# Two token tiles routed ahead in a one-core layer of attention, retention and experts

## The chip, the cores and the metric

The kernel is one program on one core of a Trainium2 chip. Its time is what the device needs for one execution, in microseconds, and the figure given for a kernel is the median of several runs. The engines are TensorE (PE, with its weight loads PEld), VectorE (DVE), ScalarE (ACT), GpSimd (POOL) and SyncE (SP), which here only issues transfers. All synchronisation is by semaphores written out by hand.

## What is computed

One layer over 512 tokens of width 1024, in float32: a norm, one input projection, windowed attention with sinks (8 heads) beside chunkwise retention (4 heads), an output projection added to the input, a second norm, and a mixture of 16 gated experts. Each token picks one group of four experts and then two experts in that group:

```python
p_group = jax.nn.softmax(hf @ rg_w + rg_b, axis=-1)
g_prob, g_idx = lax.top_k(p_group, 1)
e_logits = (hf @ re_w + re_b).reshape(-1, N_GROUPS, EXPERTS_PER_GROUP)
sel = jnp.take_along_axis(e_logits, g_idx[:, :, None], axis=1)[:, 0]
top_p, top_i = lax.top_k(jax.nn.softmax(sel, axis=-1), TOP_K_IN_GROUP)
w = g_prob * top_p / jnp.sum(top_p, axis=-1, keepdims=True)
for e in range(N_EXPERTS):          # w becomes combine[:, e]
    y = (jax.nn.silu(h @ w_gate[e]) * (h @ w_up[e])) @ w_down[e]
    out = out + combine[:, e:e + 1] * y
```

A final norm follows. Ties go to the lower index.

## The kernel before

The 512 tokens are four tiles of 128 (T = 4). Every large product is done in three passes for float32 accuracy: each weight piece is split into a high part (ACT, `hi_ring`) and a low part (DVE, `lo_ring`), and `triple` (lines 1436 to 1438) multiplies high by high, high by low and low by high. Two rings of three slots hold the split weights; the raw weights arrive through SP in twelve slots of 1 MB.

The work up to the experts follows one list, `STEPS`: pairs (weight block g, token tile t). Each engine walks the same list and puts its own side work at the steps named by tables. The last eight steps alternate the two blocks of the second half of the output projection, tile by tile: (13,0), (14,0), (13,1), (14,1), ... (14,3). After block 14 of a tile, DVE adds the product to the residual (line 1190, `x2_ready`), ACT squares it and takes a root (lines 778 to 786), PE turns the four 128x128 pieces (`turn_x2`, line 1443), ACT copies them out of PSUM (line 769), and PE multiplies them by the router's weights (`logits`, line 1611, 20 columns: 4 groups and 16 experts). DVE scales the residual into the rows of the second norm (`norm2`, line 1138), and POOL writes them to DRAM (line 543), from where the experts' rows are gathered.

The routing itself starts when the logits of all four tiles stand. It is one chain over DVE, PE and POOL: DVE finds the best group and expert, takes it out, finds the second (`first_max`, lines 1232 to 1236, twice), forms the two one-hot tables (line 1249) and their sum `pair_any` (line 1253). PE multiplies that by a triangle of ones and by ones (lines 1694, 1696): the rank of each token in its expert's list. DVE reads the rank of each choice (lines 1259, 1261) and marks it in a row of 128 (`at_rank`, line 1263, four times). PE multiplies the marks by `records`, which hold the row numbers (line 1255), and so makes the lists of each expert (`list_fields`, line 1706). DVE moves them to `meta` (line 1267, `lists_ready`), and POOL gathers the rows of experts 0 and 1 from DRAM (line 550) once the lists and all four writes of rows are there (`h2_out`). PE turns the gathered rows, lists the weights of the choices the same way, and begins the first product of expert 0. Between these steps PE runs products that nobody reads, `keep_clock` (line 1451, 128x512), so that it stays busy.

The order is fixed by hand: each engine runs its instructions as the code writes them, and waits only on semaphores. The expert stage then repeats one step of six weight blocks for each expert.

## Time and profile before

| | us |
| --- | --- |
| median of 3 runs | 565.18 |
| lowest, highest | 564.01, 565.33 |
| the profiled execution, its own time | 563.17 |
| span of its instructions | 561.1 |
| routing, from the last logits to the first product of expert 0 | 240.92 to 258.42 |

| engine | busy us | share of the span |
| --- | --- | --- |
| PE | 541.8 | 97% |
| DVE | 422.4 | 75% |
| ACT | 354.9 | 63% |
| POOL | 121.9 | 22% |

The span runs from the first to the last instruction; 2.07 us of the profiled execution lie outside it. The share of PE counts the products that nobody reads, so that a busy PE in the routing is no sign of useful work. In the chain of waits each row is the time until the next step of the chain starts.

### The profile page before, as it was taken

To read this page: it belongs to the slowest core of one execution; us is meant where nothing else is said; L and a number is where in the kernel's file an instruction comes from. 1 tells how busy PE (TensorE), PEld (TensorE's weight loads), DVE (VectorE), ACT (ScalarE), POOL (GpSimd) and SP (SyncE) were. 2 spreads that over 40 slices of the span, in tenths; PEclk is the share of its full clock that TensorE was granted. 3 is DMA by queue.
4 is the path that set the end of the run, shared out by engine and by line. 5 is a ranking of instruction groups with operands and counts; after the bars stand their busy time and mean duration, and the time that the engine had idled before them with its cause. 6 is when DMAs were issued, how large, how long until landed. Compare 5 with 4: busy or idle time off the path is not lost.

```text
span 561.1 us, 7892 instructions
## 1 busy us (share of the span) xinstructions
PE 541.8 (97%) x2679; PEld 439.7 (78%) x2680; DVE 422.4 (75%) x574; ACT 354.9 (63%) x472; POOL 121.9 (22%) x109
## 2 busy tenths in 40 slices
PE   4999999999999999988999999999999999999995
PEld 3988777777877888867888888888888888888883
DVE  3563599555856742486888898888988898888986
ACT  5563554780335352443788787788778788787854
POOL 2360000000000000020441334323442334420420
PEclk9999999999999999997999999999999999999998
DMA  8999122323020237859999999999999999999595
GB/s 291 375 304 387 33 73 76 75 77 76 0 76 0 77 113 265 292 202 323 347 387 372 370 369 373 374 346 364 356 390 373 357 365 376 381 364 373 124 210 182
DMA packets 71963, 144.02 MB, mean 257 GB/s; under 512 B 3784, under 2 KB 13312, under 8 KB 71808
## 3 DMA queue, kind: packets, MB, share of 16 engines
q1 hardware_dynamic: 64816, 120.77, 61.9%
q0 software_dynamic: 7120, 22.90, 13.4%
q8 instruction: 15, 0.25, 0.2%
q14 instruction: 12, 0.10, 0.1%
HBM read 132.77 MB, written 14.30 MB: 262 GB/s over the span
## 4 chain that ended last, share of the span: by engine, by line
PE 91%; DVE 3%; DMA 2%; ACT 2%; issue 1%; POOL 0%; DVEq 0%; POOLq 0%
PE ps L1436 25%; PE ps L1438 25%; PE ps L1437 25%; PE ps L1443 7%; PE ps L1586 2%; PE ps L1572 2%; PE ps L1548 1%; PE ps L1611 1%; PE ps L1518 1%; DMA arena<-norm_g 1%; DMA arena<-h_dram,meta 1%; PE ps L1451 1%; PE ps L1456 1%; PE ps L1808 1%; PE ps L1706 0%
## 5 line engine op out<-in xcount | busy, mean ns | idle before, releaser
L1202 DVE TENSOR_TENSOR lo_ring<-arena,hi_ring 128x2048 fp32r<-128x2048 f32 x94 | 215.3, 2291 | 29.9 <-ACT hi_ring L859 28.7
L1436 PE MATMUL ps<-hi_ring,act_hi 128*128 128x512 f32 x576 | 232.7, 404 | 0.2 <-DVE act_lo L1127 0.2
L1438 PE MATMUL ps<-hi_ring,act_lo 128*128 128x512 f32 x576 | 225.6, 392 | 0.0
L1437 PE MATMUL ps<-lo_ring,act_hi 128*128 128x512 f32 x576 | 225.0, 391 | 0.0
L859 ACT ACTIVATE hi_ring<-arena 128x2048 fp32r<-128x2048 f32 x94 | 180.1, 1916 | 21.5 <-PE ps L1438 21.5
L1436 PEld LDWEIGHTS ps<-hi_ring,act_hi 128*128 128x128 f32 x576 | 108.7, 189 | 25.7 <-issue 5.0
L1438 PEld LDWEIGHTS ps<-hi_ring,act_lo 128*128 128x128 f32 x576 | 108.4, 188 | 23.7
L1437 PEld LDWEIGHTS ps<-lo_ring,act_hi 128*128 128x128 f32 x576 | 108.7, 189 | 20.3
L969 DVE SCALAR_TENSOR_TENSOR lo_ring<-arena,over,hi_ring 128x512 fp32r<-128x512 f32 x40 | 29.3, 748 | 30.4 <-ACT hi_ring L678 30.2
L581 POOL DMA_INDIRECT y_dram<-y,row_info x14 | 15.2, 1088 | 134.3 <-issue 134.3
L979 DVE TENSOR_TENSOR act_lo<-ps,act_hi 128x512 fp32r<-128x512 f32 x56 | 36.9, 683 | 8.2 <-ACT act_hi L708 5.1
L1443 PE MATMUL ps<-keep,arena 128*128 128x128 f32 x268 | 37.5, 281 | 3.0 <-DMA arena<-h_dram,meta 2.5
L1443 PEld LDWEIGHTS ps<-keep,arena 128*128 128x128 f32 x268 | 31.8, 144 | 8.9 <-DMA arena<-h_dram,meta 2.9
L575 POOL DMA_INDIRECT arena<-h_dram,gather_idx x14 | 33.2, 2375 | 25.4 <-issue 25.4
L540 POOL DMA_DIRECT2D arena<-norm_g x1 | 0.6, 558 | 155.9 <-PE ps L1443 155.9
L598 POOL COPY row_info<-meta 128x3 int32 (+1 forms) x16 | 29.3, 1833 | 4.0 <-DMA y_dram<-y,row_info 4.0
L678 ACT ACTIVATE hi_ring<-arena,over 128x512 fp32r<-128x512 f32 x40 | 27.6, 718 | 0.5 <-DMA arena<-w_in 0.5
L881 ACT ACTIVATE act_hi<-ps 128x512 fp32r<-128x512 f32 x15 | 9.0, 599 | 21.7 <-PE ps L1443 21.7
L876 ACT ACTIVATE act_hi<-ps 128x512 fp32r<-128x512 f32 x30 | 16.3, 597 | 10.0 <-PE ps L1443 10.0
L1436 PE MATMUL ps<-act_hi,hi_ring 128*128 128x256 f32 (+1 forms) x64 | 21.9, 343 | 0.2 <-DVE lo_ring L969 0.2
L1438 PE MATMUL ps<-act_hi,lo_ring 128*128 128x256 f32 (+1 forms) x64 | 21.5, 336 | 0.0
L1437 PE MATMUL ps<-act_lo,hi_ring 128*128 128x256 f32 (+1 forms) x64 | 21.5, 336 | 0.0
(229 smaller groups left out, 533.6 us busy)
## 6 DMA issues: line engine op xcount, KB each, us to landing
arena<-w_gate SPq DMA_DIRECT2D x32, 1024.0 KB, 14.9
arena<-w_up SPq DMA_DIRECT2D x32, 1024.0 KB, 15.4
arena<-w_down SPq DMA_DIRECT2D x32, 1024.0 KB, 14.7
arena<-w_in SPq DMA_DIRECT2D x16, 512.0 KB, 10.4
y_dram<-arena POOLq DMA_DIRECT2D x8, 512.0 KB, 11.5
res<-y_dram POOLq DMA_DIRECT2D x8, 512.0 KB, 9.7
arena<-w_in SPq DMA_DIRECT2D x3, 1024.0 KB, 12.7
res<-x SPq DMA_DIRECT2D x4, 512.0 KB, 8.0
```

Of the source, the lines that this page charges most:

```text
L575: by_length(e, lambda n: pool.indirect_dma_start(x_rows[b][0:n, :], None, h2_dram, bass.IndirectOffsetOnAxis(ap=gather_idx[0:n, b:b + 1], ...
L598: nc.gpsimd.tensor_copy(row_info[:, 4 * b:4 * b + 3], meta[:, bass.ds(e * 4, 3)]).then_inc(info_ready, 1)
L678: ins = nc.scalar.activation(dst, src, ACT.Copy, scale=gain)
L859: nc.scalar.activation(hi(N1 + n12), raw(n12), ACT.Copy).then_inc(hi_done, 1)
L876: nc.scalar.activation(xt[1 - b][0][:, 4 * a:4 * a + 4, :], ps[:, 4 + a, :].rearrange("p (k s) -> p k s", k=4), ACT.Copy).then_inc(x_hi, 1)
L969: ins = nc.vector.scalar_tensor_tensor(dst, src, gain, src_hi.bitcast(F32), ALU.mult, ALU.subtract)
L979: nc.vector.tensor_tensor(dst, ps[:, bank, :].rearrange("p (k s) -> p k s", k=4), src_hi.bitcast(F32), ALU.subtract).then_inc(done, 1)
L1202: nc.vector.tensor_tensor(lo(N1 + n12), raw(n12), hi(N1 + n12).bitcast(F32), ALU.subtract).then_inc(lo_done, 1)
L1436: nc.tensor.matmul(dst, a_hi, b_hi, start=start, stop=False)
L1437: nc.tensor.matmul(dst, a_hi, b_lo, start=False, stop=False)
L1438: return nc.tensor.matmul(dst, a_lo, b_hi, start=False, stop=stop)
L1443: ins = nc.tensor.transpose(ps[:, bank, i * P:(i + 1) * P], blk, ident)
```

## The change

Four things change, all in the stretch between the last projection and the first expert.

First, the routing is split in two. `gate(0, 2)` works on tiles 0 and 1 and stands on DVE in the step (13,3), before the last tile's products are done; `find_ranks(0, 2)` and the first marks follow before the last `norm2`. `gate(2, 4)`, `find_ranks(2, 4)` and the other marks follow for tiles 2 and 3. On PE the ranks go into two banks, 1 for the early tiles and 2 for the late ones, and the lists are added up tile by tile.

Second, the experts are chosen by one table: for each five fours of logits (the groups, and four experts in each group) all 4 by 4 differences are taken, compared with a table `later` that settles ties, and summed. A logit that none beats has count 0, the second has 1. Four times the group's count plus the expert's is below 2 for the two chosen.

Third, the products of one-hot tables and row numbers go from DVE to POOL (`index_records`), in four instructions instead of two. The first two stand ahead of the last write of rows on POOL's queue, the other two behind it.

Fourth, PE's fillers are 3, 2, 1 and 21 where they were 4, 4, 15, 6 and 14, and the last two before the first product are gone. The four splits of block 16's weights all stand behind the lists now; two of them stood before.

```diff
-            for t in range(T):
+            def index_records(i, t0, t1):
+                pool.wait_ge(hot_ready, i)
+                for f in range(2):
+                    nc.gpsimd.tensor_tensor(records[:, :, t0:t1, :, f], pair_tiles[:, :, t0:t1, :],
+                                            index_tiles[:, :, t0:t1, f:f + 1].to_broadcast([P, 2, t1 - t0, E]),
+                                            ALU.mult).then_inc(index_ready, 1)
+
+            for t in range(T - 1):
                 pool.wait_ge(h2_ready, t + 1)
                 pool.dma_start(h2_dram[t * P:(t + 1) * P, :], h2_buf[t % 2]).then_inc(h2_out[t % 2], 16)
+            index_records(1, 0, EARLY)
+            pool.wait_ge(h2_ready, T)
+            pool.dma_start(h2_dram[(T - 1) * P:, :], h2_buf[(T - 1) % 2]).then_inc(h2_out[(T - 1) % 2], 16)
+            index_records(2, EARLY, T)
...
+            def gate(t0, t1):
+                n = (t1 - t0) * GROUPS
+                shape = [P, n, PER_GROUP, PER_GROUP]
+                dve.wait_ge(lg_ready, T + t1)
+                for t in range(t0, t1):
+                    ins = nc.vector.scalar_tensor_tensor(lg[:, t, :, :].rearrange("p g j -> p (g j)"),
+                                                         ps[:, 6, t * N_LOGITS:(t + 1) * N_LOGITS], rms[:, T + t:T + t + 1],
+                                                         rbias[:, :], ALU.mult, ALU.add)
+                step_done(ins)
+                v = lg[:, t0:t1, :, :].rearrange("p t g j -> p (t g) j")
+                over_v = route[:, 0:n * 16].rearrange("p (g j i) -> p g j i", j=PER_GROUP, i=PER_GROUP)
+                step_done(nc.vector.tensor_tensor(over_v, v.unsqueeze(2).to_broadcast(shape),
+                                                  v.unsqueeze(3).to_broadcast(shape), ALU.subtract))
+                step_done(nc.vector.tensor_tensor(over_v, over_v, later_v.unsqueeze(1).to_broadcast(shape), ALU.is_gt))
+                step_done(nc.vector.tensor_reduce(beaten[:, t0:t1, :, :].rearrange("p t g j -> p (t g) j"), over_v,
+                                                  AX_X, ALU.add))
+                for t in range(t0, t1):
+                    ins = nc.vector.scalar_tensor_tensor(
+                        standing[:, t, :, :], beaten[:, t, 0, :].unsqueeze(2).to_broadcast([P, N_GROUPS, PER_GROUP]), 4.0,
+                        beaten[:, t, 1:, :], ALU.mult, ALU.add)
+                step_done(ins)
+                if t0 == 0:
+                    nc.vector.memset(pair_any[:, T * E:], 0.0)
+                flat = route[:, 320 + t0 * E:320 + t1 * E]
+                nc.vector.tensor_scalar(pair_any[:, t0 * E:t1 * E], flat, 2.0, None, ALU.is_lt).then_inc(pair_ready, 1)
+                pairs = [P, 2, (t1 - t0) * E]
+                nc.vector.tensor_tensor(pair_hot[:, :, t0 * E:t1 * E], flat.unsqueeze(1).to_broadcast(pairs),
+                                        order[:, 0:2].unsqueeze(2).to_broadcast(pairs), ALU.is_equal
+                                        ).then_inc(hot_ready, 1)
...
                 if (g, t) == (N1 - 2, T - 1):
-                    for piece in range(2):
-                        split_piece(N1 + 1, piece)
+                    gate(0, EARLY)
...
+            find_ranks(0, EARLY, ps[:, 1, 0:EARLY * E])
+            mark(0)
             norm2(T - 1)
-            dve.wait_ge(lg_ready, 2 * T)
...
+            gate(EARLY, T)
+            mark(1)
+            find_ranks(EARLY, T, ps[:, 2, 0:(T - EARLY) * E])
+            for t in range(EARLY, T):
+                mark(t)
             dve.wait_ge(lists_made, 1)
...
-            for piece in range(2, 4):
+            for piece in range(4):
                 split_piece(N1 + 1, piece)
...
+                if n == T + EARLY:
+                    pe.wait_ge(pair_ready, 1)
...
             turn_x2(2 * T - 1)
-            keep_clock(4, 0)
+            for t in range(EARLY):
+                nc.tensor.matmul(late, ones_b, pair_v[:, t:t + 1, :].to_broadcast([P, T - EARLY + 1, E]), start=(t == 0),
+                                 stop=False)
+            keep_clock(3, 0)
             logits(2 * T - 1)
-            keep_clock(15, 0)
...
+            pe.wait_ge(index_ready, 2)
+            pe.wait_ge(onehot_ready, 1)
+            list_fields(7, 0, 0, True, False)
+            pe.wait_ge(pair_ready, 2)
...
+            pe.wait_ge(index_ready, 4)
+            for t in range(EARLY, T):
+                pe.wait_ge(onehot_ready, t + 1)
+                ins = list_fields(7, 0, t, False, t == T - 1)
+            ins.then_inc(lists_made, 1)
+            keep_clock(21, 0)
...
             pe.wait_ge(weights_set, 2)
-            list_fields(3, 2).then_inc(weights_made, 1)
-            keep_clock(2, 0)
+            for t in range(T):
+                ins = list_fields(3, 2, t, t == 0, t == T - 1)
+            ins.then_inc(weights_made, 1)
```

The first place is DVE from the last tile's add to the last mark. `y_68` is the scratch of the routing (`route`), `over` holds the logits, `res` the residual, `arena` the rows of the second norm, `act_lo` the marks and records. Before:

```order
L1190 TENSOR_TENSOR res<-res,ps 128x512 [waits mm_done]
L975 RECIPROCAL stat<-stat 128x1 [waits root_done]
L1138 SCALAR_TENSOR_TENSOR arena<-res,stat,arena 128x1024 [waits h2_out1,dve_step]
L1241 SCALAR_TENSOR_TENSOR over<-ps,stat,rbias 128x20 [waits lg_ready]
L1241 SCALAR_TENSOR_TENSOR over<-ps,stat,rbias 128x20 x3
L1232 TENSOR_REDUCE y_68<-over 128x20 [waits dve_step]
...
L1259 TENSOR_TENSOR y_68<-y_68,ps 128x128 [waits rank_ready]
L1261 TENSOR_REDUCE y_68<-y_68 128x8 [waits dve_step]
L1263 TENSOR_TENSOR act_lo<-keep,y_68 128x256 [waits dve_step]
L1263 TENSOR_TENSOR act_lo<-keep,y_68 128x256 x3
```

And now, from the same add:

```order
L1270 TENSOR_TENSOR res<-res,ps 128x512 [waits mm_done]
L1209 TENSOR_TENSOR y_68<-y_68,ps 128x2x32 [waits hot_ready,rank_ready]
L1211 TENSOR_REDUCE y_68<-y_68 128x2x2 [waits dve_step]
L1214 TENSOR_TENSOR act_lo<-keep,y_68 128x2x128 [waits dve_step]
L992 RECIPROCAL stat<-stat 128x1 [waits root_done]
L1155 SCALAR_TENSOR_TENSOR arena<-res,stat,arena 128x1024 [waits h2_out1,dve_step]
L1179 SCALAR_TENSOR_TENSOR over<-ps,stat,rbias 128x20 [waits lg_ready]
L1179 SCALAR_TENSOR_TENSOR over<-ps,stat,rbias 128x20
L1185 TENSOR_TENSOR y_68<-over 128x160 [waits dve_step]
L1187 TENSOR_TENSOR y_68<-y_68,keep 128x160 [waits dve_step]
L1188 TENSOR_REDUCE y_68<-y_68 128x40 [waits dve_step]
...
```

The ranks and the mark of the early tiles now stand between the add and the last norm, and the gate of the late tiles is nine instructions where the gate of all four was nineteen.

The second place is PE from the last but one set of logits. `keep,res` is a turn of the residual, `rw,arena` the logits, `hi_ring` alone a filler, `y_68,count_w` the ranks, `act_lo` alone the lists. Before:

```order
L1451 MATMUL ps<-hi_ring 128x512 x4
L1611 MATMUL ps<-rw,arena 128x20 [waits x2_copied]
L1611 MATMUL ps<-rw,arena 128x20 x3
L1451 MATMUL ps<-hi_ring 128x512 x15
L1694 MATMUL ps<-y_68,count_w 128x80 [waits counts_set,pair_ready]
...
L1451 MATMUL ps<-hi_ring 128x512 x6
L1706 MATMUL ps<-act_lo 128x32 [waits onehot_ready] x8
L1451 MATMUL ps<-hi_ring 128x512 x14
```

And now:

```order
L1485 MATMUL ps<-hi_ring 128x512 x2
L1734 MATMUL ps<-act_lo 128x32 [waits onehot_ready,index_ready]
L1734 MATMUL ps<-act_lo 128x32
L1743 MATMUL ps<-y_68,count_w 128x48 [waits pair_ready]
...
L1734 MATMUL ps<-act_lo 128x32 [waits onehot_ready]
L1734 MATMUL ps<-act_lo 128x32
L1485 MATMUL ps<-hi_ring 128x512
L1734 MATMUL ps<-act_lo 128x32 [waits onehot_ready,index_ready]
...
L1485 MATMUL ps<-hi_ring 128x512 x21
```

Three fillers stand between the last logits and the lists where 21 stood, and seven more stand behind the lists. The lists wait for POOL (`index_ready`) as well.

The third place is POOL around the last write of rows. Now:

```order
L556 DMA h_dram<-arena 128x1024 [waits h2_ready] x3
L550 TENSOR_TENSOR act_lo<-y_68,norm_tmp 128x2x2x16 [waits hot_ready]
L550 TENSOR_TENSOR act_lo<-y_68,norm_tmp 128x2x2x16
L559 DMA h_dram<-arena 128x1024 [waits h2_ready]
L550 TENSOR_TENSOR act_lo<-y_68,norm_tmp 128x2x2x16 [waits hot_ready]
L550 TENSOR_TENSOR act_lo<-y_68,norm_tmp 128x2x2x16
L567 DMA arena<-h_dram,meta 128x1024 [waits lists_ready,h2_out1,h2_out0]
```

Before, the four writes followed each other with nothing between them and the gather.

## Rows read from the trace of the kernel before

**Rows 1.** The page's chain that ended last: shares of the span by engine.

```profile
PE 91%; DVE 3%; DMA 2%; ACT 2%; issue 1%; POOL 0%; DVEq 0%; POOLq 0%
```

**Rows 2.** The chain of waits through the routing: start us, us, what.

```profile
240.92 0.69 DVE over L1241 x4
...
245.22 0.21 PE ps L1694
...
247.01 1.08 PE ps L1706 x8
248.12 0.20 DVE meta L1267
...
249.19 4.65 DMA arena<-h_dram,meta
253.89 1.97 PE ps L1443 x8
255.86 1.52 PE ps L1706 x8
257.38 1.04 PE ps L1451 x2
258.42 0.43 PE ps L1436
```

**Rows 3.** Timeline of DVE: start us, us, line, operation, tiles, shapes, idle before.

```profile
233.24 0.68 DVE L964 TENSOR_TENSOR lo_ring<-arena,hi_ring 128x512 fp32r<-128x512 f32 x1
...
236.91 0.69 DVE L1190 TENSOR_TENSOR res<-res,ps 128x512 f32<-128x512 f32 x1 [0.33 <-PE ps L1438]
...
245.56 0.29 DVE L1259 TENSOR_TENSOR y<-y,ps 128x128 f32<-128x128 f32 x1
...
246.20 1.43 DVE L1263 TENSOR_TENSOR act_lo<-keep,y 128x256 fp32r<-128x256 f32 x4
```

**Rows 4.** Timeline of ACT at the last tile, and its first SiLU later.

```profile
238.39 0.30 ACT L786 ACTIVATE stat<-stat 128x1 f32<-128x1 f32 x1
239.17 0.59 ACT L769 COPY arena<-ps 128x512 f32<-128x512 f32 x1 [0.49 <-PE ps L1443]
...
265.04 0.60 ACT L904 ACTIVATE silu_g<-ps 128x512 f32<-128x512 f32 x1 [0.80 <-PE ps L1438]
```

**Rows 5.** Line 543 in the window 240 to 241.5: the last write of rows.

```profile
DMA to landing us min/median/max: 5.6/5.6/5.6
```

**Rows 6.** Timeline of POOL at that write.

```profile
240.50 0.53 POOL L543 DMA_DIRECT2D h_dram<-arena  x1 [6.34 <-DVE arena L1138]
```

**Rows 7.** Groups of POOL by form: shapes, count | busy us, mean ns | idle before.

```profile
L598 POOL COPY row_info<-meta 128x3 int32 x10 | 19.9, 1994 | 0.0
...
L505 POOL MEMSET arena<- 128x256 int32 x1 | 0.4, 357 | 0.0
```

**Rows 8.** Windows of 1 us: busy of PE, PEld, DVE, ACT, POOL, then granted clock.

```profile
251.00:252.00 1.00, 0.37 (x2) 0.00 (x0) 0.83 (x7) 1.00 (x1) 1.00 (x2) 1.00 0.48 70
...
254.00:255.00 1.00, 1.00 (x5) 1.00 (x6) 0.00 (x0) 0.00 (x0) 0.00 (x0) 0.50 0.91 295
...
260.00:261.00 1.00, 1.00 (x5) 0.83 (x4) 0.86 (x9) 0.00 (x0) 0.00 (x0) 0.72 1.05 406
```

**Rows 9.** Timeline of PE: the 14 fillers behind the lists.

```profile
247.93 3.44 PE L1451 MATMUL ps<-hi_ring 128*128 128x512 f32 x14
```

**Rows 10.** Timeline of DVE in the first expert's step.

```profile
259.33 0.18 DVE L1296 TENSOR_REDUCE meta<-ps 128x16 f32<-128x32 f32 x1
...
262.98 0.19 DVE L1321 CAST over<-y 128x48 int32<-128x48 f32 x1
...
269.69 1.28 DVE L979 TENSOR_TENSOR act_lo<-ps,act_hi 128x512 fp32r<-128x512 f32 x2
```

**Rows 11.** The chain of waits at the second turn of rows, at the full clock.

```profile
267.67 0.87 PE ps L1443 x8
```

**Rows 12.** Line 859, ACT's high parts of the experts' weights: what ended its idle time.

```profile
  PE ps L1438: 21.5, 47
```

More of the change, by code:

```diff
@@ new lines, in find_ranks @@
+            def find_ranks(t0, t1, ahead):
+                last = t1 == T
+                dve.wait_ge(rank_ready, 2 if last else 1)
+                dve.wait_ge(hot_ready, 2 if last else 1)
+                cols = slice(t0 * E, t1 * E)
+                step_done(nc.vector.tensor_tensor(picked[:, :, cols], pair_hot[:, :, cols],
+                                                  ahead.unsqueeze(1).to_broadcast([P, 2, (t1 - t0) * E]), ALU.mult))
+                step_done(nc.vector.tensor_reduce(rank_tiles[:, :, t0:t1], picked_tiles[:, :, t0:t1, :], AX_X, ALU.add))
@@ L1141, in _, with mark @@
+            def mark(t):
+                nc.vector.tensor_tensor(at_rank[:, t::T, :], order.unsqueeze(1).to_broadcast([P, 2, P]),
+                                        rank_tiles[:, :, t:t + 1].to_broadcast([P, 2, P]),
+                                        ALU.is_equal).then_inc(onehot_ready, 1)
             for g, t in STEPS:
@@ L1681, in _ @@
             pe.wait_ge(lo_done, split_value(N1))
-            keep_clock(4, 0)
+            pe.wait_ge(counts_set, 2)
+            pair_v = pair_any.rearrange("p (t e) -> p t e", e=E)
+            early = ps[:, 1, 0:EARLY * E].rearrange("p (t e) -> p t e", e=E)
+            late = ps[:, 2, 0:(T - EARLY + 1) * E].rearrange("p (t e) -> p t e", e=E)
+            nc.tensor.matmul(early, upper_b, pair_v[:, 0:EARLY, :], start=True, stop=False)
+            nc.tensor.matmul(early[:, 1:, :], ones_b, pair_v[:, 0:1, :], start=False, stop=True).then_inc(rank_ready, 1)
@@ L1710, in _, with list_fields @@
-            list_fields(7, 0).then_inc(lists_made, 1)
-            keep_clock(14, 0)
+            keep_clock(2, 0)
+            def list_fields(bank, f, t, start, stop):
+                for k in range(2):
+                    ins = nc.tensor.matmul(ps[:, bank, 0:2 * E].rearrange("p (e f) -> p e f", f=2),
+                                           at_rank[:, k * T + t, :], records[:, k, t, :, f:f + 2],
+                                           start=(start and k == 0), stop=(stop and k == 1))
+                return ins
@@ new lines, in _ @@
+            pe.wait_ge(index_ready, 2)
+            pe.wait_ge(onehot_ready, 1)
+            list_fields(7, 0, 0, True, False)
+            pe.wait_ge(pair_ready, 2)
+            nc.tensor.matmul(late, upper_b, pair_v[:, EARLY:T + 1, :], start=False, stop=False)
+            for n in range(EARLY, T):
+                ins = nc.tensor.matmul(late[:, n - EARLY + 1:, :], ones_b,
+                                       pair_v[:, n:n + 1, :].to_broadcast([P, T - n, E]), start=False, stop=(n == T - 1))
```

124 lines of the change are left out of this document (44 added, 80 removed).

## The prediction

> **What bounds the kernel now.** I read the page's chain first: PE carries 91% of the span [rows 1], so the question is only where PE waits or does what nobody reads. The chain of waits in order of time shows one such stretch, the routing: from 240.92, where DVE takes the last logits, to 258.42, where expert 0 begins, the chain goes over DVE, PE, DVE, POOL's issue, a gather of 4.65 us and three PE items that run slowly [rows 2]. On either side PE is bound by its own products. So each microsecond that the first product of expert 0 comes earlier is worth one at the end, unless something in the experts gives it back.
>
> The reader should see in rows 2 four prices: 7.20 us from the logits to the lists (240.92 to 248.12), 1.07 from there to the gather (249.19), 4.65 until rows land (253.84, PE starts at 253.89), and 4.53 from there to the product (1.97 + 1.52 + 1.04). The last three are dear because the granted clock is 0.50, the level of 1.2 GHz, at 254 to 255, after PE had been busy for 0.37 us of 251 to 252 and then idle; it is back in the middle of 260 to 261 (0.72) [rows 8]. A turn of eight costs 0.87 at the full clock, 2.4 GHz [rows 11], against 1.97 here.
>
> **Part by part.**
>
> *The early gate.* It starts on DVE when the last split before it ends, 233.92 (233.24 + 0.68), and the last tile's add starts at 236.91 [rows 3]. Its cover is 2.99 us. No row shows an operation of 160 elements; 128 take 0.29 and 256 take 0.36 each (1.43 / 4) [rows 3], so I take 0.33 and 0.03 to the next. Two biased logits 0.36 (half of 0.69 [rows 2], rounded up), three operations of 160: 1.08, two small sums 0.30, a fill of 0.08, comparison 0.18, one-hot table 0.22: together 2.2 us, done by 236.1. From both sides: with 0.29 each 2.1, with 0.42 each (an unpipelined 256) 2.5. All of it is hidden, and PE's new wait before the logits of tile 2 (pair_ready) has ended 0.7 us before PE gets there at 236.88. The two splits that stood here go behind the lists; nobody reads them before the first product of block 16.
>
> *The last turn.* The four fillers ahead of it go. The early ranks take its place, about 0.3 us (the first of the five before took 0.21 [rows 2]). The add ends at 237.60, PE is free at 237.88, so the turn is done at 238.32 instead of 239.14. ACT's copy then waits only for ACT itself: the root starts at 238.39 and holds it for 0.2 [rows 4], so the copy runs from 238.60, not 239.17, and the logits are ready at 240.08, not 240.90.
>
> *The early ranks and mark on DVE* come before the last norm: 0.25 + 0.25 + 0.40 from 237.85, done by 238.78. The norm starts then instead of at 238.72, since the root is not ready earlier. So the last write of rows goes out at 240.56 instead of 240.50 [rows 6]. Queued behind this wait are the norm, the write and the late gate; the wait is for PE's 0.3 us of ranks, and if it were 0.5 longer all three would be 0.5 later.
>
> *The late gate* starts at 240.26, when DVE is through with the norm, not at 240.92. 0.36 + 1.08 + 0.30 + 0.18 gives pair_ready at 242.2 and the one-hot table at 242.4. Mark 1, ranks on PE (0.3), two operations of 64 elements (0.5), two marks (0.36 + 0.42 [rows 3]) end at 244.05; PE's last two list products and the way back take 0.49 as before, so DVE writes the lists at about 244.5 instead of 248.12: 3.6 us earlier.
>
> *What is late next.* POOL gathers only when the four writes have landed. The last goes out at 240.56 and takes 5.6 us [rows 5]: 246.16. Before, that was over 2.15 us before the lists (248.31) and cost nothing; now the lists stand at 244.7 and wait for it. So of the 3.6 us only 248.31 − 246.16 = 2.15 are won; POOL's issue (0.87 from the lists' end to 249.19 [rows 2]) stays behind either. With the writes no later than the lists it would be 3.6, the upper end; with the landing 1 us later, 1.15.
>
> *POOL's four multiplies.* No row has a two-input operation on POOL. From below, nothing: the sum stays. From above, the 1.99 us of COPY 128x3 [rows 7], which includes time in which it stands. The nearest row is MEMSET 128x256 at 0.36; I take 0.4 each. The first two have from 236.2 to 240.3, 4.1 us, ahead of the write: hidden at either end (4.0 at the upper). The last two start at 242.5 and are done at 243.3, before the marks; at the upper end at 246.5, the lists at 246.9, 0.8 behind the writes, and the gain is 0.8 smaller.
>
> Rows 7 show a copy of three elements on POOL at 1.99 us, about the 2.29 of the DVE operation that runs beside it in this kernel, against 0.36 for a fill of 256 when DVE was quiet. So POOL is held by DVE. Here the DVE operations beside it last 0.22 to 0.42, so a hold costs at most 0.4 each, and DVE's mark can be held as long. The Trainium skill says so too (SBUF — State Buffer, "Who interferes with whom"): a DVE instruction with two SBUF inputs and a GpSimd instruction that reads SBUF block each other wholly, whichever starts first. By that rule each side loses up to 0.4 twice and the lists come at 245.3, still ahead of the writes. [...]
>
> *Behind the gather.* Rows land at 253.89 − 2.2 = 251.7 (2.15, and 0.05 for the wait's own start). Then the turn, the list of weights and no fillers. The two fillers were 1.04 [rows 2]: all won, because x_lo was there before PE had ended the list. DVE needs the weights' records: from 244.5 with the 4.6 us it took before and 1.5 for two more splits and wider operations, 250.6, which is hidden (PE wants them at 252.6).
>
> *The clock* fell after PE's 14 fillers [rows 9] had run out, at 251.37, 2.5 us before the rows [rows 8]. Now 21 fillers start at about 244.6. At 0.24 each (3.44 / 14 is 0.246, the last one's end included [rows 9]) they end at 249.6, a gap of 2.1, nearly as before. But ahead of them PE has from 240.7 to 244.6 only one filler and the short products of ranks and lists, with waits between them: 3.9 us of thin work. I expect the clock to fall there, in most executions; some of the 21 then take 0.43, as the same shape did at the low level [rows 2]; they end between 250.7 and 252.3, and so bring the clock back and cover the gap. Then turn, list and first products run at the full clock: turn 1.97 − 0.87 = 1.10, list 1.52 − 1.08 = 0.44, and five products at 0.43 and one at 0.29 that become 0.23: 1.04 [rows 2, 8, 11].
>
> *Given back.* Behind its lists DVE has 3.83 us of small operations (259.33 to 263.16) [rows 10] and a split of 2.2 ahead of them; ACT's first SiLU waits for their end. Before, it waited for PE instead (265.04) [rows 4]. At the full clock PE reaches that point at 253.65 + 24 x 0.229 = 259.15, DVE at 260.15: 0.9 late, against a margin of 0.16 at the fourth product (269.69 + 1.28 against 271.13) [rows 10]. So 0.75 us is lost.
>
> Sum: 2.2 + 1.04 + 1.10 + 0.44 + 1.04 − 0.75 = 5.1 us. The profiled execution took 563.17 (561.1 span and 2.07 around it), which gives 558.1. The median of the runs, 565.18, is 2.0 above it; the same gain there gives 560.1, and that is the forecast for a median.
>
> **Rivals.**
>
> *The clock is low at the gather as before.* For it: a gap of 2.1 us against 2.5, if the fillers run at the full clock. Then turn and list cost what they did, products slow from 255.2 until some 258.4 instead of 2.1 us, 0.5 more. 2.2 + 1.04 − 0.5 = 2.8 less: 562.4.
>
> *The multiplies are slow.* Near 2 us each, with DVE held besides: 0.8 to 2 us less than the forecast, 561 to 562.
>
> *The gain is hidden by the weights' loads.* The experts' loads are issued at PE's pace, and ACT never waited for one (47 waits, all for PE [rows 12]), so this would need the lead to be used up; it would end near 565.
>
> *The fillers hold PE (the other side).* The clock falls in the gap before the lists and does not come back during the fillers. 21 at 0.43 last 9.0 us, from 244.8 to 253.8; then turn and list slowly, product at 257.3, 1.1 earlier than before; but if the clock stays low through the 24 products of block 15 and 16, they cost 0.2 each more, 4.8 against 1.04 before: 563.17 + 2.7 = 565.9 in the profile's terms, 567.9 for a median. It decides from the point where the fillers end after 251.7. Against it: the clock came back at 260 to 261 [rows 8], 2 us after products of 128x512 had begun to run without a gap.
>
> **How the numbers follow.** The forecast 0.52; low clock at the gather 0.24; slow multiplies 0.08; hidden by loads or anything else 0.09; fillers 0.07. What a measurement of this kernel can tell from no change is about 0.3%, 1.7 us, so faster means below 563.5. Faster: 0.52 + 0.24 + 0.08 less 0.02 for their upper tails, 0.82; same 0.11; slower 0.07. The forecast's own range is 558 to 562 (the landing a microsecond either way, and the 2.0 between profile and median); for 8 in 10 it goes up to 563.4, which takes in the second rival and its tail, and down to 557.6.
>
> **What would show it.** DVE's gate of tiles 0 and 1 inside 233.9 to 236.9, and the last add not moved. Lists written near 244.5, and POOL's gather not before the last write has landed, near 247.0: if it starts at 245.5, the landing was not late and the gain is larger. POOL's multiplies at 0.3 to 0.5. A granted clock of 0.50 somewhere in 243 to 248, and 1.00 at the gathered rows; turns in 0.9 us. ACT's first SiLU released by DVE. The forecast is wrong if the clock is 0.50 at the rows, if the fillers end after the rows land, or if the lists come after 246.2.

## The result and the profile after

| | before, same chip | after |
| --- | --- | --- |
| median of the runs, us | 564.6 (6 runs, 562.85 to 566.10) | 559.07 (6 runs, 558.23 to 561.04) |
| the profiled execution | 563.17 | 561.04 |
| its span | 561.1 | 559.4 |
| mean granted clock of TensorE | 0.991 | 0.991 |

The ratio after to before is 0.9921, with a 95% interval of 0.9900 to 0.9941: 4.5 us faster, 3.3 to 5.6. The two medians lie 5.5 apart; three of the six runs before are those that this text began with, and the ratio is what the gain is taken from. The forecast was 560.1 in a range of 557.6 to 563.4, with 0.82 on faster. One run of the kernel before in a later series, 913.59 us at a mean clock of 0.56, is left out of all ratios and counts.

The spans differ by 1.7 us only, and the reader must not take that for the gain. The last tile's add starts at 239.25 in this profile and at 236.91 before [rows 3]. Of the change only the early gate and its wait on PE stand near it, and the difference of 2.34 is not theirs: the chain of waits shows 2.28 of it at the start of the kernel already. Ten early fillers take 2.43 us in the one and 1.31 in the other, and the first low part of an activation starts at 20.29 against 18.01. Chain of waits of the kernel after, window 0 to 30; columns are start, duration and what:

```profile
13.20 2.43 PE ps L1490 x10
...
20.29 0.69 DVE act_lo L996
```

The same view of the kernel before:

```profile
12.72 1.31 PE ps L1456 x10
...
18.01 0.69 DVE act_lo L979
```

Over the 14 profiles of this case (the experiments' too) that add starts anywhere from 235.87 to 239.25, whatever the kernel. So all times in the routing are taken from now on from the start of the last add; "+8.06" is 8.06 us after it. The end of the stretch is a product-bound point: the turn of eight in expert 1, at which everything that the routing won or gave back has been added up. From there to the end of the span it is 275.6 to 276.0 us in 13 of the 14 profiles; the one exception is told at its experiment (e10).

| us after the last add | before | after |
| --- | --- | --- |
| last write of rows issued | 3.59 | 3.59 |
| lists written | 11.40 | 8.06 |
| gather issued | 12.28 | 11.39 |
| turn of the gathered rows | 16.98 | 15.64 |
| first product of expert 0 | 21.30 | 17.71 |
| turn in expert 1 | 48.51 | 44.46 |

Up to the last row the kernel after is 4.05 us shorter. In the chain after, the same columns, what stood in rows 2 as a way over DVE and PE to the lists is now one DMA:

```profile
239.25 0.70 DVE res L1270
...
242.84 6.96 DMA h_dram<-arena
249.83 0.81 issue
250.64 4.21 DMA arena<-h_dram,meta
254.89 0.67 PE ps L1477 x4
255.58 0.61 ACT act_hi L916
256.21 1.29 DVE act_lo L996 x2
257.50 2.20 DVE lo_ring L1281
```

The write of the last rows, issued at 242.84, holds the gather until 249.83. The turn, the weights' list, ACT and DVE follow at once; there is no item of 1.97 and 1.52 us as in [rows 2].

DVE's timeline after (start, duration, operation, its tiles, and in brackets the wait ahead and its releaser) shows the early gate ahead of the add and the late one behind it:

```profile
236.19 0.38 DVE L1179 SCALAR_TENSOR_TENSOR over<-ps,stat,rbias 128x20 f32<-128x20 f32 x2
236.60 0.33 DVE L1185 TENSOR_TENSOR y<-over 128x160 f32<-128x160 f32 x1
...
238.06 0.22 DVE L1200 TENSOR_TENSOR y<-y,keep 128x64 f32<-128x64 f32 x1
...
242.66 0.38 DVE L1179 SCALAR_TENSOR_TENSOR over<-ps,stat,rbias 128x20 f32<-128x20 f32 x2
...
247.12 0.19 DVE L1298 TENSOR_SCALAR meta<-ps 128x32 int32<-128x32 f32 x1 [0.85 <-PE ps L1734]
```

POOL's timeline, the same columns:

```profile
238.37 0.56 POOL L550 TENSOR_TENSOR act_lo<-y,norm_tmp 128x64 fp32r<-128x64 f32 x2 [1.87 <-DVE y L1200]
...
242.84 0.59 POOL L559 DMA_DIRECT2D h_dram<-arena  x1 [3.91 <-DVE arena L1155]
244.84 0.67 POOL L550 TENSOR_TENSOR act_lo<-y,norm_tmp 128x64 fp32r<-128x64 f32 x2 [1.42 <-DVE y L1200]
...
250.64 1.11 POOL L567 DMA_INDIRECT arena<-h_dram,meta  x1 [5.13 <-DMA h_dram<-arena]
```

The two late multiplies are over at 245.51, before PE's list products that read them start (246.07, in the next view); the gather's wait of 5.13 us ends with the write, not with the lists at 247.31. PE's timeline:

```profile
246.07 1.00 PE L1734 MATMUL ps<-act_lo 128*128 128x32 f32 x4 [0.21 <-DVE act_lo L1214]
246.92 7.67 PE L1485 MATMUL ps<-hi_ring 128*128 128x512 f32 x21
254.89 1.09 PE L1477 MATMUL ps<-keep,arena 128*128 128x128 f32 x8 [0.30 <-DMA arena<-h_dram,meta]
255.74 1.04 PE L1734 MATMUL ps<-act_lo 128*128 128x32 f32 x8
```

The 21 fillers end 0.30 us before the rows; the turn takes 1.09 instead of 1.97 and the list 1.04 instead of 1.87 (both timelines). The windows of a microsecond (length; PE, PEld, DVE, ACT, POOL with their instructions; granted clock; DMA share; GB/s) say why:

```profile
244.00:245.00 1.00, 0.23 (x3) 0.14 (x3) 0.93 (x6) 0.00 (x0) 0.16 (x1) 1.00 1.06 399
...
246.00:247.00 1.00, 0.93 (x5) 0.96 (x5) 0.27 (x1) 0.00 (x0) 0.00 (x0) 0.50 1.05 406
...
252.00:253.00 1.00, 1.00 (x4) 0.78 (x4) 0.86 (x5) 0.00 (x0) 0.95 (x1) 0.72 0.42 54
...
255.00:256.00 1.00, 1.00 (x11) 1.00 (x11) 0.00 (x0) 0.42 (x1) 0.00 (x0) 1.00 1.03 307
```

PE was busy for 0.23 of 244 to 245; at 246 the clock is 0.50, the level of 1.2 GHz, and within 252 to 253, behind most of the fillers, it is back at 2.4 GHz. Before, it was low from +16.8 to +23.7, at the rows and the first products [rows 8]; now from +6.5 to +13.3, where only list products and fillers run. Last, ACT's first SiLU after:

```profile
263.51 0.60 ACT L921 ACTIVATE silu_g<-ps 128x512 f32<-128x512 f32 x1 [1.52 <-DVE over L1355]
```

It was released by PE before [rows 4] and is released by DVE's small operations now.

### The profile page after: what moved, and what is told of

Read it like the earlier page. It is cut to its first block, busy times and chain, and to the rows that moved or that the text cites. A ratio compares the mean times of both kernels' runs of the same rounds, so it can differ in the third digit from the quotient of the medians.

```text
span 559.4 us, 7872 instructions
## 1 busy us (share of the span) xinstructions
PE 541.2 (97%) x2663; PEld 438.4 (78%) x2664; DVE 422.4 (76%) x577; ACT 354.6 (63%) x472; POOL 123.6 (22%) x113
## 4 chain that ended last, share of the span: by engine, by line
PE 88%; DVE 5%; DMA 3%; ACT 2%; issue 2%; POOL 0%; DVEq 0%; POOLq 0%
PE ps L1470 25%; PE ps L1472 24%; PE ps L1471 24%; PE ps L1477 7%; PE ps L1620 2%; PE ps L1606 2%; DMA h_dram<-arena 1%; PE ps L1582 1%; PE ps L1552 1%; PE ps L1490 1%; DMA arena<-norm_g 1%; PE ps L1647 1%; DMA arena<-h_dram,meta 1%; DVE act_lo L996 1%; PE ps L1854 1%
## 5 line engine op out<-in xcount | busy, mean ns | idle before, releaser
L598 POOL DMA_INDIRECT y_dram<-y,row_info x14 | 13.3, 948 | 133.5 <-issue 133.5
```

## The experiments

Each kernel is the kernel after with one edit, unless said otherwise; "turn in expert 1" is from the last add, as in the table above. The expectations quote 44.63 and 48.67 for it, which are the chain's; the timelines, used here throughout, give 44.46 and 48.51. Medians are in us, the kernel before on the same chip behind the stroke.

**Is it the write or the lists that bounds the gather?** Doubling the work ahead of the lists, and taking the loads away from beside the write, ask this from two sides.

```diff
+for _ in range(4):                       # the late comparison, four times more
+    step_done(nc.vector.tensor_tensor(at_rank[:, EARLY::T, :], ..., ALU.is_equal))
 for t in range(EARLY, T):
     mark(t)
```

> The changed kernel with 1.8 us more on DVE between the ranks and the last marks: the mark of tile 2 is written four times more. Theory A (the gather waits for the last write of rows, not for the lists, which in the changed kernel stood 2.5 us before the write had landed): the stretch from the last add to the turn in expert 1 grows by 0 to 0.4 us. Rival B (the lists set the gather): it grows by 1.8 us, to 46.4.

Measured: 559.44 / 564.24, ratio 0.9923 (0.9894 to 0.9952). The lists stand at +9.90, 1.84 later, the gather goes out at +11.52, and the expert's turn is at 45.35. POOL's timeline of it:

```profile
248.52 1.49 POOL L567 DMA_INDIRECT arena<-h_dram,meta  x1 [5.27 <-DMA h_dram<-arena]
```

Lists that are 1.84 us later move the gather by 0.13. The write is the bound. (The turn in expert 1 is 0.89 later, more than the 0.4 that was expected at most, because the fillers wait for the list products: they start at 246.50, last 7.22 us and end at +16.72, so that PE takes the rows late.)

```diff
 # SP, in the loop that issues the experts' loads
+if n == RING1 + 4:
+    for b in range(2): sp.wait_ge(h2_out[b], 16 * T // 2)
```

> The changed kernel with one more wait on SP: the two loads for the up weights of expert 1 start only when all four writes of rows have landed. Theory A (the last write is late because it shares the transfer engines with these two loads; alone the first write took 2.9 us, the last took 7.0): the last write lands in about 3 us, before the lists stand; the gather starts 2 to 2.5 us earlier, behind the lists. PE does not gain all of it, since its 21 fillers end 7.7 us after they start, 7.6 us behind the lists: the turn starts 0.3 us earlier, when they end. Stretch 44.3. Rival B (a write takes its 5 to 7 us whatever else moves): gather and stretch as in the changed kernel, 44.6.

Measured: 559.70 / 564.24, ratio 0.9923 (0.9898 to 0.9948). The write's landing and the gather:

```profile
DMA to landing us min/median/max: 3.0/3.0/3.0
```
```profile
248.07 1.62 POOL L570 DMA_INDIRECT arena<-h_dram,meta  x1 [2.70 <-DVE meta L1301]
```

Alone, the write lands in 3.0 us instead of 7.0, the lists release the gather, and it goes out 2.4 us earlier, at +8.95. But nothing is won (the turn in expert 1 is at 44.74), since the two loads of 1 MB then run beside the gather, which takes 6.9 us for 4.2, and the fillers stand until +15.3. Its PE timeline:

```profile
246.79 7.66 PE L1488 MATMUL ps<-hi_ring 128*128 128x512 f32 x21
255.02 1.09 PE L1480 MATMUL ps<-keep,arena 128*128 128x128 f32 x8 [0.57 <-DMA arena<-h_dram,meta]
```

So the loads are a collision that can be moved along the chain. Taking them out of the whole chain is the next edit, with fillers cut to fit:

```diff
-if n == RING2 - 2: sp.wait_ge(rows_in[0], 16)
+if n == RING1 + 4: sp.wait_ge(rows_in[0], 16)     # SP
 logits(2 * T - 1)
-keep_clock(2, 0)
+keep_clock(7, 0)
...
-keep_clock(21, 0)
+keep_clock(23, 0)
```

> The changed kernel with three edits: SP issues the loads for the up weights of expert 1 only when the first gathered rows are there, PE has 7 fillers instead of 2 ahead of the first list, and 23 instead of 21 behind the lists. Theory A (write and gather share the transfer engines with those loads; the clock falls in the routing because PE has thin work between the last logits and the lists): the last write lands in 3 us, the gather starts 8.5 us after the last add (11.4 in the changed kernel), rows land 4.2 us later, the clock stays at 1.00 throughout, product at 14.9 to 15.2 instead of 17.7. Behind it DVE's small operations still hold the SiLU, 0.9 us. Turn in expert 1 at 41.9 instead of 44.5; time 2.5 us less than the changed kernel's. Rival B (the delayed loads are then missing): ACT waits for up weights in expert 1, and the turn comes at 44 or later.

Measured: 557.17 / 563.76, ratio 0.9882 (0.9861 to 0.9904). Write 2.9 us, gather out at +8.59, rows turned at +13.43, first product at +15.50, expert 1 at 42.27, the clock at 1.00 throughout. POOL and ACT:

```profile
245.86 1.62 POOL L567 DMA_INDIRECT arena<-h_dram,meta  x1 [2.33 <-DVE meta L1298]
```
```profile
259.32 0.60 ACT L921 ACTIVATE silu_g<-ps 128x512 f32<-128x512 f32 x1 [1.54 <-DVE over L1355]
```

The rows are turned 2.2 us earlier, and these 2.2 are still there in expert 1. They come from the loads and not from the fillers, since e11 below, with more fillers and the loads left where they were, wins none of them. The stall of the SiLU is still there.

**Was that worth anything before?** The same SP edit alone, in the kernel before:

> The kernel before with only SP's loads held until the first rows are there. Theory A (before the change the lists set the gather, not the write): the last write lands 2 to 3 us earlier and nothing starts sooner for it; gather at 12.3 after the last add and turn in expert 1 at 48.3 to 48.5 as before. Rival B (the loads cost the kernel before as well): 1 us less or more, 47.5 or less.

Measured: 562.92 / 563.02, ratio 0.9993 (0.9974 to 1.0012). The write lands in 2.9 us and the gather goes out at +12.28 as ever: there the lists were the bound, as the prediction had it. This profile differs in another thing. Its windows at the wait and at the rows:

```profile
252.00:253.00 1.00, 0.00 (x0) 0.00 (x0) 0.44 (x2) 0.11 (x1) 0.04 (x1) 1.00 0.56 172
...
254.00:255.00 1.00, 1.00 (x12) 1.00 (x10) 0.26 (x1) 0.89 (x2) 0.00 (x0) 1.00 0.66 250
```

PE waited for 2.39 us between its 14 fillers and the rows, as in the kernel before, and this time the clock held. The turn in expert 1 is then at 45.68, not 48.51: the low clock at the rows costs the old kernel 2.8 us. This execution still took 563.69, because it lost 3.7 us again near its end: one load took 22 us, PE waited for the split of what it brought, and the clock fell to 0.50 at 544 to 546. Chain of waits, then PE's timeline:

```profile
514.57 22.38 DMA arena<-w_down
```
```profile
541.27 0.50 PE L1436 MATMUL ps<-hi_ring,act_hi 128*128 128x512 f32 x1 [1.95 <-DVE lo_ring L1202]
```

No other profile has PE wait for a split there, those of e6, e7 and e9 with the same edit on SP included. Two of the 12 runs of this kernel had a mean clock of 0.998 and took 560.74 and 561.11; the other ten had 0.991 to 0.995 and a median of 563.07.

**Is the low clock during the fillers itself a cost?** More fillers ahead keep PE busy:

```diff
-keep_clock(2, 0)
+keep_clock(7, 0)
...
-keep_clock(21, 0)
+keep_clock(34, 0)
```

> The changed kernel with 7 fillers instead of 2 ahead of the first list and 34 instead of 21 behind the lists, nothing else. Theory A (write sets the gather, fillers set the clock): clock 1.00 from the last add on, gather at 11.1 to 11.6 as in the changed kernel, product at 17.7, turn in expert 1 at 44.4 to 44.9; of the runs fewer are slow, since the clock no longer falls at the rows. Rival B (the low clock in the routing itself costs): the turn comes 0.5 us or more earlier, at 44.0 or less.

Measured: 559.62 / 563.02, ratio 0.9942 (0.9924 to 0.9961). In the profile the clock is 1.00 throughout the routing, the gather goes out at +11.51, the first product comes at +17.72 and the expert's turn at 44.50. That is the table's column of after within 0.12; only the lists stand 0.36 earlier, and wait for the write. So a low clock that falls on fillers and waits cost nothing here. (In four of the 12 runs the mean clock was 0.994 and not 0.997 or 0.998; where it fell in them no profile shows.)

Beside e10 this run prices the change without the clock. With the clock held, and a gather that goes out when it did (+12.28 and +11.5), the old routing reaches expert 1 at 45.68 and the new one at 44.50: 1.2 us for the two tiles ahead, the table of comparisons, POOL and the two fillers together. The other 2.8 of the 4.05 are the clock, which was low at the rows before and is low over the fillers now.

**Do the fillers decide where the clock is?**

```diff
-keep_clock(21, 0)
+keep_clock(14, 0)
```

> The changed kernel with 14 fillers behind the lists instead of 21. Theory A (the number of fillers decides the clock at the rows): at the low level they end 6 us after they start, 2 us before the rows; the clock is 0.50 or falls again at the rows or in the first products, so turn, list and six to eight products cost 1 to 2.5 us more. The stall behind DVE goes, so the turn in expert 1 comes 0.3 to 1.7 us later, at 44.8 to 46.2. Rival B (the clock at the rows does not hang on them): 44.5.

Measured: 561.44 / 563.76, ratio 0.9960 (0.9942 to 0.9979). PE:

```profile
243.78 6.21 PE L1485 MATMUL ps<-hi_ring 128*128 128x512 f32 x14
251.77 1.09 PE L1477 MATMUL ps<-keep,arena 128*128 128x128 f32 x8 [1.78 <-DMA arena<-h_dram,meta]
```

Fourteen end 1.78 us before the rows. The first product is as early as in the kernel after (+17.74), but the clock is low a second time, from +17.0 to +20.4, and the turn in expert 1 is at 45.21. This profile is of the fastest of the 12 runs (558.57, mean clock 0.988). Six others had 0.985 or 0.986 and a median of 561.95, against 560.20 for the six from 0.988 up, so the profile shows less than the usual loss. The median is 2.3 us above that of the kernel after (e12's series, another chip; by the ratios 0.3 to 0.4% of the time). It lies 2.3 us below the one before, so the longer run of fillers is a part of the gain, not all.

**What are the smaller parts worth?** The two fillers behind the weights' list, taken out of the kernel before:

```diff
 list_fields(3, 2)
-keep_clock(2, 0)
```

> The kernel before with one edit: the two fillers ahead of the first product of expert 0 are gone. Theory A (they stood on the path, at 1.2 GHz): the product starts 1.04 us earlier and, the clock rising no earlier, some of that is lost again to slow products: from the last add to the turn in expert 1 it is 47.8 to 48.0 us against 48.5. Rival B (they covered a wait for the low parts): no change, 48.5.

Measured: 562.72 / 563.76, ratio 0.9975 (0.9953 to 0.9997). The first product is 1.17 us earlier (0.18 of it because the rows came earlier), the turn in expert 1 is at 47.82, 0.69 earlier. PE:

```profile
255.20 1.97 PE L1443 MATMUL ps<-keep,arena 128*128 128x128 f32 x8 [2.35 <-DMA arena<-h_dram,meta]
...
258.53 0.77 PE L1436 MATMUL ps<-hi_ring,act_hi 128*128 128x512 f32 x1
```

The multiplies by GpSimd, given back to DVE:

```diff
-index_records(...)                       # POOL, both
+index_on_dve(0, EARLY)                   # DVE, ahead of mark(0)
+dve.wait_ge(hot_ready, 2); index_on_dve(EARLY, T)     # ahead of mark(1)
```

> The changed kernel with the row numbers multiplied by DVE again, two instructions for the early tiles ahead of the first mark and two for the late ones ahead of mark 1. Theory A (lists have slack behind the write): DVE has 0.45 us more before the norm, so the last write goes out 0.45 us later and the gather with it; the 0.45 behind the late gate is hidden. Stretch 45.1. Rival B (POOL's multiplies hold the write or the lists): it gets no longer, 44.6 or less.

Measured: 559.16 / 564.24, ratio 0.9915 (0.9889 to 0.9941). The last write goes out 0.15 later, the lists stand 0.39 later, and the gather, at +11.60, still waits for the write:

```profile
248.85 1.16 POOL L565 DMA_INDIRECT arena<-h_dram,meta  x1 [7.33 <-DMA h_dram<-arena]
```

The turn in expert 1 is at 44.94, 0.48 later: 0.21 for the gather's start, and the gather itself took 4.5 us for 4.2. The medians (559.16 here, 559.07 and 559.10 in the two series of the kernel after) tell no difference. In this kernel the move of the multiplies to POOL is worth nothing that can be measured.

**Is the SiLU's stall real, and can it go?** DVE's split of the third weight block, which stands behind the rows' low parts in both kernels, put ahead of them:

```diff
+split(2, 2)
 rows_lo(0, 1)
-split(2, 2)
```

> The changed kernel with one edit: DVE's split of the third weight block stands ahead of the low parts of the gathered rows, in the 2.8 us in which DVE idled for them (253.40 to 256.21). Theory A (the new bound behind the routing is DVE's run of small operations, which holds ACT's first SiLU): the small operations end about 2.2 us earlier, the SiLU is released by PE again, and from the last tile's add to the turn of rows in expert 1 (44.63 us in the changed kernel, 48.67 before) it is 43.8 us, 0.8 us less. Rival B (the stall at the fourth product is the rows' own path, turn to high part to low part): the stretch stays at 44.5 to 44.7, because that path is unchanged.

Measured: 560.38 / 564.24, ratio 0.9925 (0.9900 to 0.9950). The SiLU is released by PE, as theory A expected, yet the turn in expert 1 comes at 45.77, not earlier. ACT and the windows:

```profile
263.32 0.60 ACT L921 ACTIVATE silu_g<-ps 128x512 f32<-128x512 f32 x1 [0.81 <-PE ps L1472]
```
```profile
250.00:251.00 1.00, 1.00 (x6) 0.82 (x5) 0.83 (x6) 0.13 (x1) 0.70 (x2) 1.00 0.00 0
...
256.00:257.00 1.00, 0.93 (x3) 0.81 (x3) 0.96 (x5) 0.00 (x0) 0.18 (x1) 0.50 1.37 274
```

The clock came back early, in 3.4 us instead of 6.8, so the 21 fillers ran faster (6.66 us) and ended 2.1 us before the rows, and the clock fell again at the first products. I could not tell whether the split did that, so the kernel after was run once more:

> The changed kernel itself, once more, beside the others on one chip. Theory A: in its profile the last write lands in about 7 us and the gather starts 11.1 to 11.6 after the last add; the turn in expert 1 at 44.4 to 45.8, the upper end where the clock falls at the rows. Median 0.5 to 0.9% under the kernel before. Rival B (the 7 us was chance): it lands in 5.6 as in the profile of before, gather at 10.1, turn at 43.2.

Measured: 559.10 / 563.02, ratio 0.9928 (0.9901 to 0.9955). Its profile does the same without any edit: low from +7.3 to +10.7, fillers over at +13.94 and rows at +15.88, and low again from +17.5 to +20.9. Windows:

```profile
250.00:251.00 1.00, 1.00 (x6) 0.82 (x5) 0.86 (x6) 0.00 (x0) 0.69 (x2) 1.00 0.00 0
...
256.00:257.00 1.00, 1.00 (x3) 0.71 (x3) 1.00 (x2) 0.00 (x0) 0.00 (x0) 0.50 0.93 223
```

There the turn in expert 1 is at 45.56 and the SiLU is released by PE: with the products slow, DVE is in time by itself. So e1 tells nothing of the stall, since the clock had taken it away already. The kernel after has two ways to run, 4.05 and 2.95 us ahead of the kernel before in the routing.

The combination of the split with the loads behind the rows and the fillers of e6:

> As loads_behind_rows, and DVE's split of the third weight block ahead of the low parts of the rows. Theory A (small operations hold the SiLU): 0.8 us less than without, turn in expert 1 at 41.1. It can be less: rows land sooner here, so DVE may have less idle time ahead of them, and a split that is not done when the rows come costs up to 1 us at the first product. Rival B: as e6 or up to 1 us more.

Measured: 558.85 / 563.76, ratio 0.9917 (0.9892 to 0.9943), worse than without the split. The rows come at +13.53, but the split holds DVE when it should write the rows' low part; the first product is 0.96 later than in the kernel without it (+16.46), the clock, at 1.00 until then, falls at +16.4, and the turn in expert 1 is at 44.22 for 42.27. PE's busy share in the windows of the wait and of the fall:

```profile
252.00:253.00 1.00, 0.04 (x1) 0.00 (x0) 1.00 (x3) 0.00 (x0) 0.00 (x0) 1.00 0.53 176
...
254.00:255.00 1.00, 1.00 (x4) 0.71 (x4) 0.90 (x8) 0.00 (x0) 0.00 (x0) 0.50 0.75 250
```

The stall must be taken out of DVE at a place where nobody waits for DVE. The six small operations that compute where the results go need only the lists:

```diff
+# the six slot operations: picked, place_kt, ..., slot_idx (slots_ready)
 rows_lo(0, 1)
...
-# the six slot operations, here until now
```
(with the loads behind the rows and 7 and 23 fillers, as above)

> loads_behind_rows with one more edit: of DVE's small operations, the six that set the slots of the records (0.98 us) stand ahead of the low parts of the rows, in the 1.05 us in which DVE idled there. Theory A (DVE's small operations hold the SiLU and by it the fourth product): the product starts as before at 15.5 after the last add or 0.1 later, the SiLU is released by PE, the turn in expert 1 comes 0.7 us earlier, at 41.6. Rival B (the clock or another path decides): 42.3 or more.

Measured: 556.82 / 563.02, ratio 0.9910 (0.9876 to 0.9944). The last slot operation, 251.49, ends beside the start of the rows' low part; the SiLU is released by PE, and the turn in expert 1 is at 41.52, 0.75 earlier than with the stall. DVE, then ACT:

```profile
251.49 0.17 DVE L1333 CAST slot_idx<-y 128x8 int32<-128x8 f32 x1
251.56 1.28 DVE L996 TENSOR_TENSOR act_lo<-ps,act_hi 128x512 fp32r<-128x512 f32 x2
```
```profile
258.16 0.60 ACT L921 ACTIVATE silu_g<-ps 128x512 f32<-128x512 f32 x1 [0.80 <-PE ps L1472]
```

By its profile and its median this is the best version of the case: 2.3 us below the kernel after on the same chip (556.82 against 559.10), 6.2 below the kernel before. Its ratio says less, 5.1 us, as one of its six runs took 561.28. The 0.75 shows in the profile; between e6 and e9, medians 557.17 and 556.82 and ratios 0.9882 and 0.9910 on different chips, it can't be told.

## Why the prediction was right, and its largest wrong term

**The early gate and turn.** Early gate 2.1 us for 2.2, all ahead of the add, which no line moved. ACT's copy starts at 238.59 for 238.60, where it stood at 239.17 before [rows 4] (times after with the 2.34 of the start taken off, here and below). Right.

**The late gate.** Started at 240.32 for 240.26, one-hot table at 242.40 for 242.4, marks over at 243.92 for 244.05. Lists at 244.97 for 244.7: the 0.27 are the list products, which ran at the low clock; they had been costed at the full one.

**What is late next.** The mechanism was right, the size was not. The gather waits for the last write and not for the lists (e2, e3). But the step "takes 5.6 us: 246.16" took 7.0. That 5.6 was one execution: in eight other profiles with the two loads beside the write it took 6.7 to 7.4, in five without them 2.9 to 3.0. Only one of the eight (e5, 6.8) has the old routing, so how much of the 1.4 was a low draw and how much the new order brought isn't shown; the third write, for which nobody waits, took 5.9 and 7.0 us in the old routing and 8.9 to 10.2 in the new one. So the gather went out 0.89 us earlier, not 2.15, and less than the 1.15 that the prediction had as its lower end. The gather itself then took 4.2 us instead of 4.65, which nobody had forecast and which makes 1.34 at the rows. This term was 0.9 too large.

**POOL's multiplies.** Three of the four took 0.30 or 0.31 us and one 0.41 (the same 0.41 in e2, e6, e11 and e12), for 0.4, and all are hidden. The one of 0.41 is the first of the late pair, which starts at 244.84 beside DVE's mark (244.67 to 245.09); the early pair had DVE idle beside it. So a hold of 0.1 us shows, not the 0.4 that was allowed for, and DVE's mark took the same 0.42 as the early one. The Trainium skill's GPSIMD Engine Reference ("Elementwise") has 4497 ns for 2048 elements; by the element an estimate for 64 is 0.14, and the trace's 0.30 lies above it. The rival of slow multiplies is out, and e4 shows that the place of these operations does not matter here.

**Fillers and clock.** The clock fell in the routing, as expected: at +6.4 to +7.5 in all seven profiles that have two fillers ahead of the lists, and not there in any of the four that have seven. The 21 fillers outlasted the thin part: 7.67 us, over 0.30 us before the rows. Then the turn took 1.09 for 1.97, the list 1.04 for 1.87 and the first products ran at 2.4 GHz. So it went in the first profile. The second profile (e12) shows the rival in part: fillers over 1.94 us too soon and the clock low at the first products, though not at the turn. The chance of 0.24 for a low clock was needed; that it comes at the products, 2 us later, had not been foreseen, nor that the choice between the two is made anew in each execution. The rival of fillers that hold PE did not come; they ended before the rows in both profiles of this kernel.

**Given back.** 0.75 expected, and the SiLU was to be released by DVE: it is, and ACT is idle for 1.52 ahead of it, against 0.80 where PE releases it at the same clock (e9), so 0.72 late; e9 is 0.75 shorter than e6. (In the prediction's own terms, 260.15 against 259.15, it would have been 1.0 late and not 0.9.) It exists only while the clock holds, and then in the old routing too: in e10 ACT is idle for 1.41 until DVE. So it is the price of the clock and not of the change.

**The sum.** Predicted 5.1 us; the stretch gives 4.05 and 2.95 in the two profiles, and 0.4 comes on top outside the span. The terms of the first: 1.34 at the rows, 2.25 from the rows to the first product (4.32 before, 2.07 after, where 1.04 + 1.10 + 0.44 = 2.58 had been expected), and 0.46 from there on (27.21 before, 26.75 after, where 1.04 − 0.75 = 0.29 had been expected). Of the missing 0.33 of the second, PE waited 0.18 for x_lo, which the prediction had held for ready and the two fillers had covered; by the starts in PE's timelines turn and list together gave 1.44 instead of 1.54, and the fillers had taken 0.99, not 1.04. Of the fillers' gain a part goes again behind: in e5, 1.17 at the first product was 0.69 in expert 1.

The 0.4 is a term that the prediction held fixed. It added 2.07 us around the span before and after. In every run of the old routing the time of an execution is 2.0 to 2.2 us above its span, and in every run of the new one, experiments included, 1.6 to 1.8. Why isn't shown. With it the first way makes 4.05 + 0.43 = 4.5 us and the second 3.4, and the ratio says 4.5 (3.3 to 5.6).

The clocks of all runs help to weigh the ways. Of 53 runs of the kernel before, in the three series of experiments, 49 had a mean clock of 0.991 or 0.992 and four had 0.996 to 0.999; these four took 559.80, 559.94, 560.46 and 562.13, and the median of all 53 is 563.56. The mean doesn't say where the clock was low, but it fits an old routing that loses the clock at the rows in about 9 executions of 10, at some 3 us, as e10's profile has it (2.8). The kernel after, over its two series of six, has a median of 559.07 at a mean clock of 0.990 to 0.992 throughout: it too loses the clock each time, but over fillers. Its two ways have the same mean clock, since the clock is low for 6.8 us in the one and twice for 3.4 in the other. So which of them is the more frequent stays open. The single median of 559.07 against 564.60 flatters the change by a microsecond.

So the number is near in part by luck: a write that was 1.4 slow was met by a gather that was 0.4 fast and by 0.4 outside the span, and neither had been forecast. The measured median is even 1.0 below the forecast, though the gain was 0.6 smaller. And the split of the routing was not tried alone: no run has it without the new table of comparisons or with the old fillers between, so their shares in the 1.2 us of e11 against e10 are not shown.

## What to carry to other kernels

When a computed result stops being the last of several things that an instruction waits for, the second to last becomes the price: look up its own duration in more than one profile before taking it for fixed, and ask what runs beside it. A transfer of half a megabyte on the critical path is worth moving megabyte loads out of its way, but only as far as the whole chain of transfers goes, or the collision just moves. Work that fills a wait must be sized to end when the wait ends, at either level of the clock. And where the clock falls in most executions, compare the two kernels with the clock held in both as well: here only 1.2 us of the 4.05 belong to the shorter chain.

## What the runs showed of the hardware

- A write of the last rows took 2.9 to 3.0 us without two loads of 1 MB beside it (five profiles) and 5.6 to 7.4 with them (nine); the first gather took 4.0 to 4.9 without such loads and 6.9 beside them (e3).
- The granted clock fell while PE was still working, thinly: busy for 0.23 of 244 to 245, at 0.50 by 246. In the same kernel it stayed low for 6.8 us in one execution and for 3.4, twice, in another. With PE's wait for the rows at 2.52 and 2.35 us it fell in two executions of the old routing (before, e5), and at 2.39 it held in a third (e10).
- Code ahead of the routing took up to 3.4 us more or less from one execution to the next (last add at 235.87 to 239.25). In three of the 14 profiles the ten early fillers took 2.43 us instead of 1.31, and these have the three latest adds (238.40, 239.12, 239.25), although the granted clock of the windows from 8 to 20 stands at 1.00 in them as in the others; why isn't shown. A comparison of spans of single profiles would have read 1.7 us where the routing had won 4.
